# Branch projections on upper and lower parts, retention one chunk ahead, constants loaded inside the stages

## The reference

```
# first block
z = rmsnorm(x, g_mix) @ w_in
h_m  = two-way mLSTM        (width 512)
h_na = neighbourhood attention (width 256)
h_mem = attention to 256 memory tokens (width 256)
gates = sigmoid(gate_pre).reshape(b, s, 3, 1024)
y = gates[0] * (h_m @ w_proj_mlstm) + gates[1] * (h_na @ w_proj_na) + gates[2] * (h_mem @ w_proj_mem)
x = x + y @ w_out
x = x + square(relu(rmsnorm(x, g_ffn) @ w_up)) @ w_down
# second block
proj = rms_norm(x, attn_norm) @ w_in_2
o_a = gated_delta_net(...)                       # 4 heads of 128
# retention, 4 heads of 128, chunk by chunk:
attn = (q @ k.T) * decay;  o = attn @ v + q_dec @ state
state = state * chunk_decay + k_dec.T @ v
o_b = rms_norm(o, norm_b) * silu(gate)
x = x + concat(o_a, o_b) @ w_out_2
x = x + hierarchical_moe(rms_norm(x, ffn_norm))  # 64 experts, 2 per token
return rms_norm(x, final_norm)
```

## Time and profile before

| | |
|---|---|
| median of 3 runs | 3181.86 us (3181.43 to 3188.68) |
| profiled execution | 3181.37 us, span 3179.6 us |
| TensorE busy, by records | 2848.5 us (90%) |
| VectorE / ScalarE / GpSimd busy | 1275.7 / 576.6 / 346.7 us |
| mean granted clock of TensorE | 0.956 |
| branch stage | about 533 to 914 us |
| retention, then the transposing stage | about 2343 to 2405, 2405 to 2428 us |
| routing and experts | about 2546 to 3138 us |

### The profile page before, as it was taken

The page is one execution under the profiler, slowest core; times in us unless marked ns, Lnnn a source line. Parts: engine busy times, 40 slices in busy tenths (PEclk is TensorE's granted clock), DMA queues, the critical chain, the costliest instruction groups (busy, mean ns, idle before and its releaser), DMA issues. The chain is left out here.

```text
span 3179.6 us, 41994 instructions
## 1 busy us (share of the span) xinstructions
PE 2848.5 (90%) x17256; PEld 2184.2 (69%) x17256; DVE 1275.7 (40%) x2182; ACT 576.6 (18%) x1424; POOL 346.7 (11%) x486
## 2 busy tenths in 40 slices
PE   7987888999999999999998998899987958888883
PEld 5866755777777888888887886777876835555551
DVE  5657376222244524343344653554424341111114
ACT  3232176000002101000002422330020201111111
POOL 1013200000001000000001002540020111111112
PEclk9989999999999999999999999999998969999996
DMA  3120120111130111111114220002102179999994
GB/s 129 54 83 21 50 93 25 53 37 53 33 112 28 53 53 40 53 49 58 40 53 103 45 41 1 2 2 67 47 10 91 73 296 413 415 413 408 401 369 196
DMA packets 131742, 362.89 MB, mean 114 GB/s; under 512 B 14808, under 2 KB 61016, under 8 KB 114144
## 3 DMA queue, kind: packets, MB, share of 16 engines
q1 hardware_dynamic: 119456, 342.35, 30.0%
q0 software_dynamic: 10512, 16.80, 1.4%
q10 hardware_dynamic: 1584, 1.05, 0.1%
HBM read 349.21 MB, written 31.52 MB: 120 GB/s over the span
## 5 line engine op out<-in xcount | busy, mean ns | idle before, releaser
L454 PE MATMUL banks<-hT_upper,split_weights 128*128 128x512 f32 x2304 | 744.8, 400 | 14.8 <-PEq L204 8.8
L454 PEld LDWEIGHTS banks<-hT_upper,split_weights 128*128 128x128 f32 x2304 | 434.9, 189 | 116.7 <-issue 22.1
L445 PE MATMUL banks<-split_weights,hT_upper 128*128 128x512 f32 x1536 | 484.2, 397 | 23.4 <-DVE hT_lower L137 9.9
L454 PE MATMUL banks<-hT_lower,split_weights 128*128 128x512 f32 x1152 | 450.4, 391 | 0.0
L445 PEld LDWEIGHTS banks<-split_weights,hT_upper 128*128 128x128 f32 x1536 | 291.8, 191 | 86.6 <-issue 19.5
L445 PE MATMUL banks<-split_weights,uT_upper 128*128 128x512 f32 x1024 | 315.6, 389 | 0.0
L2960 PE MATMUL banks<-expert,ex_xT 128*64 128x256 f32 (+1 forms) x1632 | 261.7, 397 | 47.6 <-DMA expert<-in_w_up 22.8
L445 PE MATMUL banks<-split_weights,hT_lower 128*128 128x512 f32 x768 | 303.8, 396 | 0.0
L454 PEld LDWEIGHTS banks<-hT_lower,split_weights 128*128 128x128 f32 x1152 | 217.6, 189 | 54.9 <-issue 11.2
L2960 PEld LDWEIGHTS banks<-expert,ex_xT 128*64 128x64 f32 (+1 forms) x1632 | 170.9, 149 | 102.7 <-issue 60.4
L445 PEld LDWEIGHTS banks<-split_weights,uT_upper 128*128 128x128 f32 x1024 | 192.0, 188 | 39.6
(11 more groups left out here) (473 smaller groups left out, 3581.0 us busy)
## 6 DMA issues: line engine op xcount, KB each, us to landing
expert<-in_w_gate SPq DMA_DIRECT2D x51, 1024.0 KB, 14.9
expert<-in_w_up SPq DMA_DIRECT2D x51, 1024.0 KB, 22.0
expert<-in_w_down SPq DMA_DIRECT2D x51, 1024.0 KB, 24.5
raw_weights<-in_w_in SPq DMA_DIRECT2D x38, 1024.0 KB, 5.4
raw_weights<-in_w_up SPq DMA_DIRECT2D x16, 1024.0 KB, 5.3
raw_weights<-in_w_down SPq DMA_DIRECT2D x16, 1024.0 KB, 5.0
hT<-in_w_gate SPq DMA_DIRECT2D x13, 1024.0 KB, 11.6
hT<-in_w_up SPq DMA_DIRECT2D x13, 1024.0 KB, 23.0
```

The lines of the kernel that those rows point to most:

```text
L445: last = pe.matmul(bank, acts[x][:, r * KT // 2 + k, m * P:(m + 1) * P].bitcast(F32R), w[y][:, k, :].bitcast(F32R), start=(r == 0 and k == ...
L454: last = pe.matmul(out, w[x][:, k, c0:c0 + P].bitcast(F32R), acts[y][:, k, t0:t0 + nt].bitcast(F32R), start=(k == 0 and x == y), stop=(k = ...
```

## The change

The gate chunks and the units of the branch stage go branch by branch. Its projections are made in three passes: activations and projection weights are split too, the lower part in the place of the whole. The projection weights have one place. A unit is four gates, then four projections.

In the retention, keys and queries are turned and copied one chunk ahead, the finish of a chunk comes behind the mask of the next one, and turning both halves of the mixed output, with its two parts, is done inside the loop; the stage `transpose_tokens` is gone. Keys and queries, turned, lie in the raw weight buffer.

Constants are placed ahead and loaded by SyncE at the start of the stage that uses them, or, for the routing, during `project_norm` into the raw buffer. ScalarE issues one load of down weights, that of expert 61 in the order, that SyncE issued before. The diff, cut to its core:

```
-    out += [cols(w1, IN1["branch"] + b * D + n * HALF, HALF) for n in range(4) for b in range(3)]
+    out += [cols(w1, IN1["branch"] + b * D + n * HALF, HALF) for b in range(3) for n in range(4)]
...
+def place_later(c, mem, sizes):
+
+    c.awaited = place_consts(c, mem, sizes)
+
+
+def place_in_raw(c, at, sizes):
+
+    flat = c.raw[:, :, :].rearrange("p k n -> p (k n)")
+    for name, shape in sizes:
+        n = math.prod(shape[1:])
+        view = flat[:, at:at + n]
+        c.k[name] = view.rearrange("p (a b) -> p a b", b=shape[-1]) if len(shape) == 3 else view
+        at += n
+    c.awaited = sizes
+
+
+def load_awaited(c, sp):
+
+    for name, shape in c.awaited:
+        load_const(c, sp, name, shape, c.consts_landed)
+    c.n_consts += len(c.awaited)
+
+
+def wait_consts(c, eng):
+    eng.wait_ge(c.consts_landed, 16 * c.n_consts)
...
+            load_awaited(c, sp)
             c.load_chunks(sp, C_BRANCH + 1)
...
+                if i == 0:
+                    wait_consts(c, dve)
...
+def gated_branches(c, hT, branches, lowers, yT):
...
+    units = [(b, n) for b in range(3) for n in range(4)]
+    quarters = [(ch, th) for ch in range(2) for th in range(2)]
...
+        tiles = [w.shape[0] // P for _, w in branches]
+        at = [0, 0, tiles[1]]
+        acts_upper = c.sb(mem, "br_acts_upper", [P, max(tiles), S])
+        acts = [[acts_upper[:, at[b]:at[b] + tiles[b], :], lowers[b]] for b in range(3)]
+        pw_lower, pw = c.same_place(mem, ("br_proj_lower", "br_proj"), [P, max(tiles), HALF])
+        pw_upper = c.sb(mem, "br_proj_upper", [P, max(tiles), HALF])
...
+            for u, (b, n) in enumerate(units):
+                if u:
+                    sp.wait_ge(proj_there, 4 * u)
+                sp.dma_start(pw[:, 0:tiles[b], :],
+                             branches[b][1][:, n * HALF:(n + 1) * HALF].rearrange("(k p) n -> p k n", p=P)).then_inc(pw_there, 16)
+                c.load_chunks(sp, C_BRANCH + u + 2)
...
+            def gates(u):
+                c.wait_split(pe, C_BRANCH + u)
+                for a, (ch, th) in enumerate(quarters):
+                    if u:
+                        pe.wait_ge(gate_done, 4 * (u - 1) + a + 1)
+                    split_channels(nc.tensor, c.bank(a), hT, th * BANK, BANK, c.parts(C_BRANCH + u), ch * P).then_inc(gate_there, 1)
+
+            def projections(u):
+                b, _ = units[u]
+                pe.wait_ge(acts_split, tiles[0] + b)
+                pe.wait_ge(pw_split, u + 1)
+                for a, (ch, th) in enumerate(quarters):
+                    if u:
+                        pe.wait_ge(multiplied, 4 * (u - 1) + a + 1)
+                    split_channels(nc.tensor, c.bank(NB + a), acts[b], th * BANK, BANK, [pw_upper[:, :, :], pw_lower], ch * P,
+                                   kt=tiles[b]).then_inc(proj_there, 1)
+
+            for u in range(len(units)):
+                gates(u)
+                projections(u)
...
+            def take_acts(b):
+                n = tiles[b] if b == 0 else 1
+                for k in range(n):
+                    part = slice(k, k + 1) if b == 0 else slice(0, tiles[b])
+                    nc.scalar.activation(acts[b][0][:, part, :].bitcast(F32R), branches[b][0][:, part, :], ACT.Copy).then_inc(acts_upper_done, 1)
+
+            take_acts(0)
...
+                if i == 15:
+                    act.wait_ge(proj_there, 16)
+                    take_acts(1)
+                    take_acts(2)
...
+            def split_acts(k, upper, lower, whole):
+                dve.wait_ge(acts_upper_done, k + 1)
+                take_lower(nc.vector, lower, whole, upper).then_inc(acts_split, 1)
+
+            def split_pw(u):
+                t = tiles[units[u][0]]
+                dve.wait_ge(pw_there, 16 * (u + 1))
+                take_upper(nc.vector, pw_upper[:, 0:t, :], pw[:, 0:t, :]).then_inc(pw_upper_done, 1)
+                dve.wait_ge(pw_upper_done, u + 1)
+                take_lower(nc.vector, pw_lower[:, 0:t, :], pw[:, 0:t, :], pw_upper[:, 0:t, :]).then_inc(pw_split, 1)
...
+            for k in range(tiles[0]):
+                split_acts(k, acts[0][0][:, k, :], lowers[0][:, k, :], branches[0][0][:, k, :])
+            for i in range(4 * len(units)):
+                u, a = i // 4, i % 4
+                (b, n), (ch, th) = units[u], quarters[a]
+                if a == 0:
+                    split_pw(u)
+                    c.split_chunk(dve, C_BRANCH + u + 1)
...
+                if i == 15:
+                    for k in range(2):
+                        split_acts(tiles[0] + k, *acts[k + 1], branches[k + 1][0])
...
+                sp.wait_ge(c.split_done, j0 + 4)
+                load_awaited(c, sp)
...
-            dve.wait_ge(zeroed, 1)
-            split(dve, nc.vector, tap, c.k["w_ba"][:, :, :], w_ba[0], w_ba[1]).then_inc(wba_split, 1)
...
+                if ch == 0:
+                    wait_consts(c, dve)
+                    split(dve, nc.vector, tap, c.k["w_ba"][:, :, :], w_ba[0], w_ba[1]).then_inc(wba_split, 1)
...
+        turned_rows = c.raw[:, :, :].rearrange("p k n -> p (k n)").rearrange("p (a n) -> p a n", n=BANK)
+        kT, qdT = turned_rows[:, 0:2, :], turned_rows[:, 2:4, :]
+        attnT = c.sb(mem, "rt_attnT", [P, BANK])[:, :]
...
+            def turn_first(m):
+                if m:
+                    pe.wait_ge(s["first_lower"], m)
+                for h in range(H):
+                    last = nc.tensor.transpose(head(c.bank(3), h), head(first[:, m, :], h), c.k["ident"][:, :])
+                last.then_inc(s["first_turned"], 1)
+
+            def turn_o(m):
+                pe.wait_ge(s["o_done"], m + 1)
+                if m:
+                    pe.wait_ge(s["o_lower"], m)
+                for h in range(H):
+                    last = nc.tensor.transpose(head(c.bank(7), h), head(o[:, m, :], h), c.k["ident"][:, :])
+                last.then_inc(s["o_turned"], 1)
+
+            turn_kq(0)
...
+                if m + 1 < C:
+                    turn_kq(m + 1)
                 pe.wait_ge(s["kd"], m + 1)
-                if m:
-                    pe.wait_ge(s["state"], m)
+                pe.wait_ge(s["state"], m + 1)
...
+                turn_first(m)
...
+                if m:
+                    turn_o(m - 1)
+            turn_o(C - 1)
...
+            def copies(m):
...
+            def upper_o(m):
+                act.wait_ge(s["o_turned"], m + 1)
+                nc.scalar.activation(place(upper, 1, m).bitcast(F32R), blocks(c.bank(7)), ACT.Copy).then_inc(s["o_upper"], 1)
+
+            copies(0)
+            for m in range(C):
+                if m + 1 < C:
+                    copies(m + 1)
+                act.wait_ge(s["first_turned"], m + 1)
+                nc.scalar.activation(place(upper, 0, m).bitcast(F32R), blocks(c.bank(3)), ACT.Copy).then_inc(s["first_upper"], 1)
...
+                if m:
+                    upper_o(m - 1)
+            upper_o(C - 1)
...
+            def lower_first(m):
+                dve.wait_ge(s["first_upper"], m + 1)
+                take_lower(nc.vector, place(lower, 0, m), blocks(c.bank(3)), place(upper, 0, m)).then_inc(s["first_lower"], 1)
+
+            def lower_o(m):
+                dve.wait_ge(s["o_upper"], m + 1)
+                take_lower(nc.vector, place(lower, 1, m), blocks(c.bank(7)), place(upper, 1, m)).then_inc(s["o_lower"], 1)
...
+                if m:
+                    dve.wait_ge(s["o_there"], m)
                 nc.vector.tensor_tensor(attnT, c.bank(2), decay[:, :, :].rearrange("p h k -> p (h k)"), ALU.mult).then_inc(s["attnT"], 1)
+                if m:
+                    finish(m - 1)
+                lower_first(m)
...
-                finish(m)
+                if m:
+                    lower_o(m - 1)
+            finish(C - 1)
+            lower_o(C - 1)
...
+        released = [[i + SLOTS for i in unit if i + SLOTS < UNITS[LAST][0]] for unit in UNITS]
+        LAST_DOWN = UNITS[LAST][0] - 1
+        RELEASES_LAST = [LAST_DOWN in r for r in released].index(True)
...
+                    if i != LAST_DOWN:
+                        down(i)
...
+                if isinstance(u, int) and u == RELEASES_LAST:
+                    slot = LAST_DOWN % SLOTS
+                    act.wait_ge(down_used[slot], LAST_DOWN // SLOTS)
+                    experts.load_down(act, slot, experts.number(act, slice(LAST_DOWN, LAST_DOWN + 1)))
...
-        x_sb = c.sb(ctx, "x", [P, TT, D])
+        x_lower, x_sb = c.same_place(ctx, ("branches_lower", "x"), [P, TT, D])
...
-            retention(c, q, k, v, o_b)
-        transpose_tokens(c, "tr2", [(o_a, h_parts[1][:, 0:4, :], BANK), (o_b, h_parts[1][:, 4:8, :], BANK)],
-                         upper=[h_parts[0][:, 0:4, :], h_parts[0][:, 4:8, :]])
+            retention(c, q, k, v, o_b, o_a, h_parts[0], h_parts[1])
...
```

(4 more changed lines are left out.)

135 lines of the change are left out of this document (38 added, 97 removed).

## The result

The changed kernel takes 3114.41 us, median of four runs (3113.51 to 3116.93); the kernel before, timed beside it, 3185.27 (3181.43 to 3192.29). The ratio is 0.9776 with a 95% interval of 0.9755 to 0.9797. Forecast were 3116 us and a range of 3107 to 3138.

What follows compares the result with a forecast made beforehand. Branch stage bound by TensorE's matmuls, retention by hand-offs, experts by transfers, with stand-stills at three edges. Gains 24.3 + 28.5 + 13.4 = 66.2 us from 3181.4 give 3115.2, plus 0.5 to the median 3116 us; range 3107 to 3138.

Steps and rivals of the forecast that it cites:

- Part 1: Branch stage: projections as three-pass matmuls on split parts, 87.1 us instead of 111.7; 24.3 us gained.
- Rival (d): Branch stage: three-pass projections run at the plain record's 0.43 us, costing 78 us, 3194 us in all; chance 0.04.
- Part 2: Retention: keys and queries one chunk ahead, turning inside the loop, period 5.55 us instead of 6.91; 28.5 us gained.
- E: Retention: TensorE's free moment after a chunk's output matmuls; the first chunk's was to move from 2352.43 to 2354.1.
- Rival (a): Retention loop: hand-offs hold the period at 6.9 us, gain 19.0 instead of 28.5, 3125 us; chance 0.13.
- Rival (b): Retention loop: more transposes drop it to the lower clock, 10.6 us of TensorE per period, 3153 us; chance 0.05.
- Part 3: Three stage edges: separate constant-load blocks go, saving 2.0, 6.1 and 5.3 us, together 13.4 us.
- Rival (c): Stage edges: they keep their stand-still without the load blocks, 13.4 us less gained, 3129 us; chance 0.04.
- Part 4: Expert stage: last down weights loaded on ScalarE's queue; taken as 0, bounds 4.1 us gained, 0.5 lost.

Runs made afterwards that it cites:

- u1_plain: Changed kernel with its branch projections as 128 plain float32 matmuls again, in the new order, without the splits they no longer need: 3142.36 us.
- r6_finish: Changed kernel with the finish of the chunk before put ahead of the masked attention on VectorE again: 3128.75 us.
- r7_twice: Changed kernel with every transpose of the retention loop issued twice into the same place, matmuls unchanged: 3127.11 us.
- u9_third: Changed kernel with only the third group of constants (seven loads ahead of the routing) in a block of its own again: 3120.67 us.
- u4_down: Changed kernel with the last down weights issued by SyncE again, before the last unit, instead of on ScalarE's queue: 3114.24 us.
- u8_second: Changed kernel with only the second group of constants (ten loads ahead of the second layer's inputs) in a block of its own again: 3121.09 us.
- r5_lower: Changed kernel with VectorE taking the turned output's lower part behind the next chunk's masked attention in the retention loop: 3113.03 us.

## Why the prediction was right

**Part 1** (24.3 us): 24.0 and 24.9 by the table, where the attention stage is counted in; 24.6 from the first sigmoid to the next stage, in both profiles (369.1 to 344.5). The price per matmul was exact: the records read 0.39 us, their spacing is 0.2267. The 24.6 was put down to the form alone, and u1_plain gives 22.9 of it to the form and 1.7 to the order.

```profile
L460 PE MATMUL banks<-br_acts_upper,br_proj_upper x128: 389/389/389, 558.2 to 883.9; 128*128 128x512 f32 x128
```

Rival (d) fell. Its 0.43 was not a record's length, as the prediction has it, but the spacing of the plain product's two records (0.859 / 2); the plain record reads 0.59. The three-pass matmuls did not run at it. The splits hid: VectorE waited for projection weights to land (8.4, 5.1 and 3.7 us in ten places), and nobody waited for their parts.

**Part 2** (28.5): 28.9 and 27.7. The first chunk's E came 10.9 us after the stage's start (11.1 predicted), the period was 5.59 (5.55; the first 4.88, since nothing of a chunk before is turned in it), and the next stage's first matmul 56.5 us after the start ("some 57"). Against the earlier trace rows, the path is the predicted one step by step:

```profile
2333.49 0.28 ACT L2571 ACTIVATE rt_junk<-banks 128x128 f32<-128x128 f32 x1 [1.46 <-PE banks L2542]
...
2334.96 0.59 ACT L2559 ACTIVATE hT_upper<-banks 128x512 fp32r<-128x512 f32 x1
...
2335.65 0.69 DVE L137 TENSOR_TENSOR hT_lower<-banks,hT_upper 128x512 fp32r<-128x512 f32 x1 [1.28 <-ACT hT_upper L2559]
...
2336.26 0.68 DVE L2601 TENSOR_TENSOR rt_attnT<-banks,rt_decay 128x512 f32<-128x512 f32 x1
2336.86 1.12 DVE L2585 SCALAR_TENSOR_TENSOR x<-banks,rt_ors,x 128x128 f32<-128x128 f32 x4
...
2336.99 0.49 PE L2541 MATMUL banks<-rt_state,raw_weights 128*128 128x128 f32 x2
```

Squares, upper part at once behind them, lower part, mask, outputs. Rival (a) fell, and r6_finish shows one thing that it needed: without the finish behind the mask the period is 6.95 us. Rival (b) fell: by the profile the clock was 1.00 in the loop, and r7_twice kept it there with twice the transposes. The prediction's argument for this was weaker than it looked, since its stretch from 2411 to 2416 stops where the clock falls, and r7_twice has the same share of matmuls as the loop before. The clock's rise behind transposes alone, by 14.89 and at 39.9 in the changed kernel, is what holds. The rule of the Trainium skill (TensorE: Matmul & The Clock Gate, Part 4) that transposes don't count as activity does not agree with these rows.

**Part 3** (13.4): as lengths the edges are right (6.1 and 5.2 by the idle time before the first work; u9_third 5.5 by median). As prices they are not complete. The prediction put everything behind an edge at nothing, and behind the second one the stretch is longer or shorter with the clock: 3.4 to 10.6 us in place of 6.1. From the first profile of the kernel before to the changed kernel 2.6 of the 6.1 us went there again (610.0 against 607.4). All three groups together cost 21.9 us by median against 13.4, and the two that were taken singly 11.5 against 11.4. Rival (c) fell.

**Part 4** (0): u4_down.

**The sum.** The terms add up to 66.2 us, the profiles differ by 69.0 and 65.9, the medians by 71. That the forecast of the time came within 2 us of the median is in part luck. The kernel before was put at 3181.9, and its medians are 3185 to 3188, because the profiled execution was near its fastest (3181.37). The gain was put some 5 us too low. The two cancel. No profile shows where the medians' 5 us lie; the 8 us that the three groups of constants cost together beyond their edges point to Part 3, and this is not shown.

## What to carry to other kernels

In a loop of hand-offs, write down the path in microseconds from the rows and look for the step that stands in a queue only because it was written there: one line moved back on VectorE cost the whole shortening of the period (10.7 us), a second one moved gave 3 us more, and keys and queries a chunk ahead without the first left the period at 6.95 us. What the first is worth without them was not measured. Price a matmul by the spacing of many, never by its record. When a stand-still is taken out, its length is not yet its price: an edge of 6.1 us gave 3.4 to 10.6, and the difference went with the clock in the stages behind it. Single profiles that differ by 2 to 3 us a stage need a second profile before a cause is named.

## What the runs showed of the hardware

The first stages, the same code in every kernel, lasted from 270.1 to 275.3 us in the eleven profiles without the first group's block. Most of it follows the moment from which TensorE's clock stays at the upper level. In the changed kernel (270.1 us) the first matmuls behind the transposes run at that level:

```profile
41.28 0.40 PE L500 MATMUL banks<-hT_upper,in_w_if_upper 128*40 128x512 f32 x1 [1.05 <-PEq L226]
```

In u8_second (275.3 us) the same matmuls take 0.63 us, 0.43 apart, until 47.8:

```profile
41.80 0.62 PE L521 MATMUL banks<-hT_upper,in_w_if_upper 128*40 128x512 f32 x1 [1.05 <-PEq L247]
...
47.34 0.63 PE L521 MATMUL banks<-hT_lower,in_w_if_upper 128*40 128x512 f32 x1
...
48.27 0.39 PE L521 MATMUL banks<-hT_lower,in_w_if_upper 128*40 128x512 f32 x1
```

In all 14 profiles the mLSTM stage (GpSimd's first instruction there) starts the later, the later this rise is: 191.4 us for a rise at 39.8, 193.1 at 44.5, 193.7 at 46.2, 194.6 at 47.8. The rest of the first stages takes 78.4 to 78.7 us in six of the eleven and 80.0 to 80.7 in five. The difference is larger than those that r5_lower and u4_down were built to find, and only the stage's own length could tell them. What moves the rise from one execution to the next was not shown.

The granted clock of a stretch has to be read with care here. The view of u8_second gives 1.00 for the same time,

```profile
20.00:50.00 30.00, 20.00 (x72) 13.18 (x73) 23.69 (x29) 9.94 (x19) 7.67 (x11) 1.00 0.39 122
```
